# The down-projection of a two-mixer layer's MLP as seven half-sized products, accumulated and combined on VectorE

## The reference

```python
hn2 = rmsnorm(x, norm2_g[l])
up, ffn_new = causal_dwconv(hn2 @ w_up[l], st_ffn[l], ffn_conv_w[l])
a_f, b_f = jnp.split(up, [D_FF], axis=-1)
x = x + (jax.nn.silu(a_f) * b_f) @ w_down[l]
...
y = rmsnorm(x, norm_f_g)
```

## Time and profile before

| | before |
|---|---|
| median of 3 runs (lowest, highest) | 3739.96 us (3736.24, 3740.8) |
| profiled execution: time, span | 3742.75 us, 3741.0 us |
| mean granted TensorE clock | 0.979 of full speed |
| TensorE busy | 3574.4 us, 96% |
| VectorE busy | 2115.3 us, 57% |
| ScalarE busy | 710.3 us, 19% |
| GpSimd busy | 560.7 us, 15% |

### The profile page before, as it was taken

One profiled execution on the slowest core, in us unless ns is written; L12 is line 12 of the kernel. 1 busy time (PEld: TensorE's weight loads), 2 busy tenths in 40 slices (PEclk: granted clock), 3 DMA queues, 4 the chain that ended last, 5 costly groups with the idle time before them and its releaser, 6 DMA issues. The chain is left out here.

```text
span 3741.0 us, 49643 instructions
## 1 busy us (share of the span) xinstructions
PE 3574.4 (96%) x16817; PEld 2477.4 (66%) x16817; DVE 2115.3 (57%) x4957; ACT 710.3 (19%) x1564; POOL 560.7 (15%) x913
## 2 busy tenths in 40 slices
PE   7999999999999999999789999999989999999994
PEld 4666666666666666666567676767767777777772
DVE  2445555544455555445435656666666666666665
ACT  2222332222223322222111110101101111111112
POOL 1111100111110001111321111111132112112100
PEclk9999999999999999999779999999999999999997
DMA  5012221211122121111541111111131111111102
GB/s 194 23 46 67 67 67 56 67 47 47 52 67 67 58 65 60 45 40 60 159 149 34 50 34 47 37 45 39 34 126 52 34 40 39 39 34 45 39 22 101
DMA packets 202822, 224.04 MB, mean 60 GB/s; under 512 B 12764, under 2 KB 151556, under 8 KB 202771
## 3 DMA queue, kind: packets, MB, share of 16 engines
q1 hardware_dynamic: 202771, 223.37, 19.1%
HBM read 193.67 MB, written 29.67 MB: 60 GB/s over the span
## 5 line engine op out<-in xcount | busy, mean ns | idle before, releaser
L612 PE MATMUL mixer_bank<-arena,hnt 128*128 128x451 f32 x2176 | 923.7, 553 | 13.1 <-DVE yo L1227 9.5
L1846 PE MATMUL mlp_bank<-wd,act 128*128 128x512 f32 x1496 | 663.4, 596 | 21.2 <-DVE act L2086 21.2
L1787 PE MATMUL mlp_bank<-arena,ws 128*128 128x176 f32 (+1 forms) x3520 | 655.1, 339 | 0.2 <-ACT raw L1901 0.2
L1787 PEld LDWEIGHTS mlp_bank<-arena,ws 128*128 128x128 f32 x3520 | 587.9, 190 | 36.8 <-ACT raw L1901 0.5
L612 PEld LDWEIGHTS mixer_bank<-arena,hnt 128*128 128x128 f32 x2176 | 385.3, 191 | 302.8 <-issue 292.6
L1846 PEld LDWEIGHTS mlp_bank<-wd,act 128*128 128x128 f32 x1496 | 275.2, 186 | 354.2 <-issue 287.3
L549 POOL TENSOR_TENSOR ex<-dtt,level 128x512 f32<-128x512 f32 (+1 forms) x114 | 143.0, 1255 | 1150.6 <-DVE dtt L1432 740.2
L2072 DVE SCALAR_TENSOR_TENSOR mcv<-raw,cf,mcv 128x512 f32<-128x512 f32 (+2 forms) x440 | 289.6, 658 | 15.7
L2111 DVE TENSOR_TENSOR arena<-arena,mlp_bank 128x512 f32<-128x512 f32 (+1 forms) x396 | 263.9, 684 | 54.4 <-PE mlp_bank L1846 52.1
L628 PE MATMUL mixer_bank<-wo,th 128*128 128x512 f32 (+1 forms) x544 | 267.3, 615 | 6.4 <-DMA wo<-in_w_out_dram 6.4
L1787 PE MATMUL mlp_bank<-arena 128*128 128x176 f32 (+1 forms) x1320 | 253.4, 342 | 10.9 <-POOL ident_mlp L2008 10.1
(11 more groups left out here) (304 smaller groups left out, 3895.5 us busy)
## 6 DMA issues: line engine op xcount, KB each, us to landing
wo<-in_w_out_dram SPq DMA_DIRECT2D x272, 256.0 KB, 2.9
arena<-in_w_up_dram SPq DMA_DIRECT2D x44, 512.0 KB, 5.0
wu<-in_w_up_dram SPq DMA_DIRECT2D x44, 512.0 KB, 5.0
wd<-in_w_down_dram SPq DMA_DIRECT2D x44, 512.0 KB, 3.3
arena<-in_w_in_dram SPq DMA_DIRECT2D x8, 1804.0 KB, 17.3
xt<-in_x_prompt_dram SPq DMA_DIRECT2D x16, 512.0 KB, 3.3
xr<-in_x_prompt_dram SPq DMA_DIRECT2D x16, 512.0 KB, 3.4
resid<-yo SPq DMA_DIRECT2D x16, 512.0 KB, 3.5
```

The lines of the kernel that those rows point to most:

```text
L612: x = pe.matmul(bank[ring(g)][0:N, 0:GW], hnt[:, k, 0:N], w[:, k, g * GW:(g + 1) * GW], start=(k == 0), stop=(k == KT - 1))
L1787: x = pe.matmul(out[:, 0:N], left[:, k, :], xb[:, slot, k, g * N:(g + 1) * N], start=first and k == 0, stop=k == HK - 1, skip_group_check= ...
L1846: pe.matmul(bank[4 + (q + 2 * p * ps) % 4][0:N, :], act_[p][:, t * C:t * C + N], wd[p][:, e * 512:e * 512 + 512], start=True, stop=True).t ...
```

## The change

The down-projection is done for two steps at a time (a pair: steps 2i and 2i+1, 11 pairs in a pass). Over a pair the product is (1024 tokens x 256) by (256 x 1024); it is cut in halves in all three directions and done with seven products of half size each way instead of eight. So a pair has 28 products of the same shape as before instead of 32; the 32 sample tokens are left plain, two outputs of two accumulated products each. The 28 stand in pair i+1: 14 in its first step and 14 in its second.

The eight sums that this needs are on VectorE: `act_parts` (four, on 128 x 512 of the activations) and `weight_parts` (four, on 128 x 512 of the weights), put between the additions of `add` in the first step of a pair. The outputs accumulate over the pairs in seven sums, `acc`, which begin as three blocks of zeros and four of the residual, prepared by GpSimd (`start`). At the end of a pass they are combined (`combine`, seven additions): for half of the rows inside the last step, for the rest in `close`.

The last pair of a pass is plain: `close` does 16 (18) outputs of two products each, accumulated in PSUM, straight into the combined result. The final norm is now in both `close`s: ScalarE squares and scales tile by tile; the scaling on VectorE (`finish`) is in pass 1's `close` for its tiles, and for pass 0's in the first two steps of pass 1 (between the additions). The stores of pass 0 go out there as well. The transposes of the convolution tails (`turn_tails`) move into pass 1's `close`. `acc` takes the place of `y`; `act_` (four tiles now), `wd` and the sums are in the arena, and `wd` holds one pair.

```diff
+        PAIRS = FT // 2
+        OUTS = (28, 30)
+        CLOSING = (16, 18)
+        Q0 = (0, OUTS[0] * (PAIRS - 1) + CLOSING[0])
+        ORDER = (0, 1, 4, 5, 2, 6, 3, 7)
-        y_half = (sb("y", [C, TILES // 2, D]),
-                  arena[:, 0:(TILES // 2 + 1) * D].rearrange("p (t d) -> p t d", d=D))
+        acc = sb("acc", [C, 7, 4, 512])
+        y_sample = (sb("y_sample", [C, 512])[0:S, :], arena[0:S, 7808:8320])
+        act_ = [arena[:, i * PW:(i + 1) * PW] for i in range(4)]
+        act_sums = arena[:, 4224:5760].rearrange("p (i n) -> p i n", i=3)
+        wd_sums = arena[:, 5760:7808].rearrange("p (i n) -> p i n", i=4)
+        wd = [arena[:, 8320 + i * D:8320 + (i + 1) * D] for i in range(2)]
+        gf = act_sums[:, 0:2, :]
...
+            def down(ps, i):
+                if not (fixed(i, 1) and ps == 0):
+                    sp.wait_ge(s_down_done, first_out(ps, i))
+                for p in range(2):
+                    sp.dma_start(wd[p], w_down[bass.ds((2 * i + p) * C, C), :]).then_inc(s_wd_loaded, 16)
+
+            def start(ps):
+                if ps:
+                    sp.wait_ge(s_y_stored, 16 * 8)
+                for b in range(4):
+                    rows = slice(ps * T // 2 + b // 2 * 512, ps * T // 2 + b // 2 * 512 + 512)
+                    cols = slice(b % 2 * 512, b % 2 * 512 + 512)
+                    sp.dma_start(acc[:, 1 + b, :, :], resid[rows, cols].rearrange("(t p) d -> p t d", p=C))\
+                        .then_inc(s_acc_loaded, 16)
+                if ps:
+                    for e in range(2):
+                        sp.dma_start(y_sample[e], resid[T:T + S, e * 512:e * 512 + 512]).then_inc(s_acc_loaded, 16)
...
-                down(ps, FT - 1, 1)
+                up(ps, 3, 1)
+                with sp.Fori(2, PAIRS) as i:
+                    up(ps, sp.snap(2 * i), 0)
+                    up(ps, sp.snap(2 * i + 1), 1)
+                    down(ps, sp.snap(i - 1))
+                down(ps, PAIRS - 1)
+                sp.dma_start(gf, norm_f_g.partition_broadcast(C).rearrange("p (e d) -> p e d", e=2))\
+                    .then_inc(s_gf_loaded, 16)
+
+            def stores(ps):
+                for k, t in enumerate(ORDER):
+                    sp.wait_ge(s_f_out, 8 * ps + k + 1)
+                    r0 = ps * T // 2 + t * C
+                    sp.dma_start(y_p[r0:r0 + C, :].rearrange("p (e d) -> p e d", e=2), y_tile(t)).then_inc(s_y_stored, 16)
...
+            def down(ps, i, p, half, first, last):
+                a0, a1 = act_[2 * p], act_[2 * p + 1]
+                if first == 0 and half == 0:
+                    pe.wait_ge(s_act_made, group(ps, 2 * i + 1, PASSES[ps][1]))
+                    pe.wait_ge(s_wd_loaded, 32 * (PAIRS * ps + i + 1))
+                elif half == 0:
+                    pe.wait_ge(s_down_sums, 20 * ps + 2 * i + 2)
+                for o in range(14 * half + first, 14 * half + min(last, 14)):
+                    q, m = divmod(o, 7)
+                    lo, hi = slice(q * C, q * C + C), slice(512 + q * C, 512 + q * C + C)
+                    left, right = ((a0[:, lo], wd[0][:, 0:512]), (a1[:, lo], wd[1][:, 0:512]),
+                                   (act_sums[:, 2, lo], wd[1][:, 512:]), (a1[:, hi], wd_sums[:, 3, :]),
+                                   (act_sums[:, 0, lo], wd_sums[:, 0, :]), (act_sums[:, 1, lo], wd_sums[:, 1, :]),
+                                   (a0[:, hi], wd_sums[:, 2, :]))[m]
+                    bank_free(ps, i, o)
+                    pe.matmul(bank[4 + o % 4][:, :], left, right, start=True, stop=True).then_inc(s_down_done, 1)
+                if ps and half and last >= 14:
+                    for e in range(2):
+                        bank_free(ps, i, 28 + e)
+                        plain(bank[4 + e], 2 * p, 8, e, S)
+
+            def plain(out, a, t, e, N):
+                for j in range(2):
+                    x = pe.matmul(out[0:N, :], act_[a + j][:, t * C:t * C + N], wd[j][:, e * 512:e * 512 + 512],
+                                  start=(j == 0), stop=(j == 1))
+                x.then_inc(s_down_done, 1)
...
+            def close(ps):
+                i, o = PAIRS - 1, 0
+                pe.wait_ge(s_act_made, group(ps, FT - 1, 1))
+                pe.wait_ge(s_wd_loaded, 32 * PAIRS * (ps + 1))
+                for k, t in enumerate(ORDER + (8,) * ps):
+                    if k == 2:
+                        pe.wait_ge(s_act_made, group(ps, FT - 1, PASSES[ps][1]))
+                    for e in range(2):
+                        bank_free(ps, i, o)
+                        plain(bank[4 + o % 4], 2 * (i % 2), t, e, S if t == 8 else C)
+                        o += 1
+                    if ps and k in (1, 3, 5):
+                        turn_tails(k // 2)
+
+            def pair(ps, i, p):
+                up(ps, 2 * i if isinstance(i, int) else pe.snap(2 * i), 0, lambda: down(ps, i - 1, 1 - p, 0, 0, 2))
+                down(ps, i - 1, 1 - p, 0, 2, 14)
+                up(ps, 2 * i + 1 if isinstance(i, int) else pe.snap(2 * i + 1), 1,
+                   lambda: down(ps, i - 1, 1 - p, 1, 0, 2))
+                down(ps, i - 1, 1 - p, 1, 2, 14)
...
+            def start(ps):
+                if ps:
+                    gp.wait_ge(s_combined, 21 * ps)
+                for m in (1, 6, 7):
+                    x = gp.memset(acc[:, m - 1, :, :], 0.0)
+                x.then_inc(s_acc_step, 1)
+                gp.wait_ge(s_acc_loaded, 64 + 96 * ps)
+                gp.wait_ge(s_acc_step, ps + 1)
+                gp.tensor_tensor(acc[:, 2, :, :], acc[:, 2, :, :], acc[:, 4, :, :], ALU.subtract).then_inc(s_acc_ready, 1)
...
+            def act_parts(ps, i, p):
+                lo, hi = slice(0, 512), slice(512, 1024)
+                step = 5 * (10 * ps + i)
+                a0, a1 = act_[2 * p], act_[2 * p + 1]
+                dve.wait_ge(s_act_made, group(ps, 2 * i + 1, PASSES[ps][1]))
+                dve.tensor_tensor(act_sums[:, 0, :], a0[:, hi], a1[:, hi], ALU.add).then_inc(s_sums_step, 1)
+                dve.wait_ge(s_sums_step, step + 1)
+                dve.tensor_tensor(a0[:, hi], a0[:, lo], a0[:, hi], ALU.subtract).then_inc(s_sums_step, 1)
+                dve.tensor_tensor(act_sums[:, 1, :], act_sums[:, 0, :], a0[:, lo], ALU.subtract).then_inc(s_sums_step, 1)
+                dve.wait_ge(s_sums_step, step + 3)
+                dve.tensor_tensor(act_sums[:, 2, :], a1[:, lo], act_sums[:, 1, :], ALU.subtract).then_inc(s_down_sums, 1)
+
+            def weight_parts(ps, i):
+                lo, hi = slice(0, 512), slice(512, 1024)
+                step = 5 * (10 * ps + i) + 3
+
+                def first():
+                    dve.wait_ge(s_wd_loaded, 32 * (PAIRS * ps + i + 1))
+                    dve.tensor_tensor(wd_sums[:, 0, :], wd[0][:, hi], wd[0][:, lo], ALU.subtract).then_inc(s_sums_step, 1)
+                    dve.tensor_tensor(wd_sums[:, 2, :], wd[1][:, hi], wd[0][:, hi], ALU.subtract)
+
+                def second():
+                    dve.wait_ge(s_sums_step, step + 1)
+                    dve.tensor_tensor(wd_sums[:, 1, :], wd[1][:, hi], wd_sums[:, 0, :], ALU.subtract)\
+                        .then_inc(s_sums_step, 1)
+                    dve.wait_ge(s_sums_step, step + 2)
+                    dve.tensor_tensor(wd_sums[:, 3, :], wd[1][:, lo], wd_sums[:, 1, :], ALU.subtract)\
+                        .then_inc(s_down_sums, 1)
+                return (first,), (second,)
+
...
+            def combine(ps, n, q0, q1, steps):
+                v = [None] + [acc[:, m, q0:q1, :] for m in range(7)]
+                n += 21 * ps
+                for k in steps:
+                    to, by, done = ((6, 1, 0), (2, 1, 0), (7, 6, 1), (6, 5, 3), (3, 6, 4), (4, 7, 3), (5, 7, 4))[k]
+                    if k == 0:
+                        dve.wait_ge(s_y_added, first_out(ps, PAIRS - 2) + 14 * (q0 // 2 + 1))
+                    if done:
+                        dve.wait_ge(s_combined, n + done)
+                    dve.tensor_tensor(v[to], v[to], v[by], ALU.add).then_inc(s_combined, 1)
+
...
+            def close(ps):
+                n, o = first_out(ps, PAIRS - 1), 0
+                order = ORDER + (8,) * ps
+                for k, t in enumerate(order):
+                    N = S if t == 8 else C
+                    if k in (0, 4, 6):
+                        dve.wait_ge(s_combined, 21 * ps + (7, None, None, None, 14, None, 21)[k])
+                    for e in range(2):
+                        dve.wait_ge(s_down_done, n + o + 1)
+                        if o == 0:
                             dve.wait_ge(s_y_added, n)
-                        v = y_half[ps][0:N, t, e * 512:e * 512 + 512]
-                        dve.tensor_tensor(v, v, bank[4 + (q + 2 * p * ps) % 4][0:N, :], ALU.add)\
-                            .then_inc(s_y_added, 1)
+                        v = half_acc(t, e, N)
```

(19 more changed lines are left out.)

282 lines of the change are left out of this document (148 added, 134 removed).

## The result

| | before | after |
|---|---|---|
| median (lowest, highest) | 3740.38 us (3736.24, 3741.06), 4 runs | 3650.07 us (3649.07, 3652.91), 4 runs |
| ratio, 95% interval | | 0.9762, 0.9745 to 0.9779 |
| profiled execution: time, span | 3742.75, 3741.0 us | 3652.91, 3651.2 us |

The forecast was 3641 us with a range of 3619 to 3668, so the time lies in the range and 9 us above the forecast. The direction and most of the size are right. The question is where the 9 us are, and whether the terms were right or errors cancelled.

The account below looks back on a forecast made before the run. TensorE was taken to bound the loops, with standing at the passes' ends. Terms -68.9 + 1.4 - 0.9 + 7 - 37.9 = -99.3 us from 3742.75 give 3643.5, median 2.8 us lower: 3641 us, range 3619 to 3668.

Parts of the forecast that it names:

- Parts 1 and 2: Loops: four products fewer a pair save 68.9 us; VectorE's added sums cost 1.4 us of waiting in pass 1's second group.
- Part 3: VectorE operations with two SBUF inputs and GpSimd's SBUF reads exclude each other for a whole instruction; a sum takes 2.06 us.
- Part 4: End of pass 0: weights wait 4.9, slow clock 2.4, combinings 9, ScalarE 1, less 18.2 us; together -0.9 us.
- I take 9 us: Pass 0's `close`: cost of VectorE's 14 combining additions at 2.06 us beside GpSimd's sums, ends 0 and 14.
- The 1 us for ScalarE: Between the passes: ScalarE squares pass 0's last tile before it copies pass 1's first product, 1 us.
- the prediction's own sign: Wrong if TensorE waits over 1 us a pair in loops, or pass 0's `close` ends off VectorE's count.
- Part 5: Beginning of each pass, +7 us: pass 1's collisions with GpSimd 5, scalings of pass 0's tiles 1, pass 0's start 1.
- Part 6: End of the kernel: 56.5 us becomes 18.6, -37.9 us (ends -42 and -31), with 7.5 to the last scaling, 3.8 for the store.
- No collision at the ends: Rival, 15%: at the passes' ends VectorE's combining finds GpSimd idle and the clock stays up; 3622 us.
- VectorE paces pass 1: Rival, 17%: the second group's 0.1 us margin fails and the wait passes through convolution and gate; 3664 us.
- The products save nothing: Rival, 3%: in the loops TensorE waits for free banks instead, so only the end is won; about 3709 us.
- the likeliest case: The forecast itself for the whole kernel, 3641 us, given 63%; its own range 3626 to 3656 us.

## Why the prediction was right, and where its terms were off

**Parts 1 and 2, products and VectorE in the loops.** Right in mechanism and size: 68.7 against 68.9 us, pairs of 72.38 and 77.90 against 72.4 and 78.2. The 1.4 us of waiting in pass 1's second group (for nine pairs; there are ten) did not come; there is 0.33 us of room where the prediction had 0.1, and the run with two sums more shows that this place, not the load of 72%, would have decided.

**Part 3, GpSimd against VectorE.** Confirmed by the runs: 1.89 us for three combinings without the input sums, 5.14 with them. The Trainium skill, "SBUF — State Buffer", section "Who interferes with whom", has a VectorE instruction with two SBUF inputs and a GpSimd instruction that reads SBUF exclude each other for a whole instruction; the 4.49 us for 32 columns beside a subtraction of 4.83 us agree.

**Part 4, the end of pass 0.** The wait for the weights was 5.15 us (4.9 forecast) and the slow clock behind it 3.3 us (2.4): 48 halves in 23.86 us, at 0.4293 us each 20.6. The step "I take 9 us" for the combinings was too high: they took 1.52 us each (21.27 us for fourteen) where the prediction took 2.06 for all. The first of each group took 0.68 to 0.98 us, and only the eight behind it 1.64 to 2.16; TensorE waited 2.55 us, lost 1.9 to the clock behind it (8.79 us for 16 halves, 6.87 at 0.4293 us each), 4.5 in all, and leaving the sums out gave 4.6. The 1 us for ScalarE does not show at pass 1's first product. The rest was -5.3 instead of -0.9. By the prediction's own sign (`close` ends earlier than VectorE's count says) this part was wrong in size: VectorE's count was 39 us, and 21.3 + 10 = 31 came.

**Part 5, the beginnings of the passes, is the term that failed.** "5 us, ends 0 and 12" for pass 1 and "1 us" for pass 0. Measured, with part 2, 21.6 us instead of 8.4. The step was "in 53 to 55, GpSimd's subtraction to 60": it timed the start of the sums by the residual's landing. In the trace GpSimd's queue sets it: `keep` of the second step waits for VectorE's last addition (row at 2803.75, 15.21 us idle), and then zeroings and subtraction follow without a gap, 5.46 + 4.83 us; the residual, issued at 2792.88, was there in time. The zeroings had no price in the prediction, and the convolution of the second step, which TensorE's third step wants, falls right beside them and the subtraction; the prediction had put `act_parts` there and the convolution beside the weight sums, and it came the other way round. In pass 0 the same happens, though its residual is there early: that reason for "1 us" was beside the point. Taking the work off GpSimd gave back about 5 us in pass 0 and 6 in pass 1. Beside the 6.58 us pass 1 has costs of its own: 1.52 us at its second product, which comes from the close (0.42 us without the input sums), 1.12 us at 2790.32 behind a scaling of 2.04 us (1.28 in pass 1's close), 4.4 us at the turns of VectorE's loop, which the prediction didn't have, 2.1 us for the two waits behind the 6.58, and 1.35 of slow clock. That makes 17.1 us; less the 3 us that the ten pairs gave beyond their products, 14 of the 15.7 are found.

**Part 6, the end.** -34.3 instead of -37.9. VectorE was quicker than the 7.5 us taken (4.4), but "3.8 us for the store" was 9.1: the order of SyncE's queue was not read, though it stands in the code. With the stores first it is 4.0 us. The three transposes of the tails, now between products in `close`, had no term: TensorE's next product starts 0.65 us after the start of each, 2 us in all.

**The rivals.** No collision at the ends: wrong, the collisions are there. VectorE paces pass 1: not by this change, but 1 us more would have done it. The products save nothing: a pair is shorter by all of its four products. So the likeliest case was right. That the total was nearer than its terms is in part luck: pass 0's close and the unchanged first part were 7.5 us better than forecast while the passes' beginnings and the end were 16.8 us worse. Measured again, the kernel was 14 us above the forecast, still in its range.

## What to carry to other kernels

When set-up work is put on an idle engine, time it by that engine's queue, with what stands before and behind it, and not by its input; splitting its instructions frees the neighbour but not the queue. A transfer moved to just before a place where the bound engine waits is worth its full time only until the next wait, so look up what that is first. Price an end by the last engine's queue of stores, in its order. A loop that goes over twice as many steps may pay at each turn: compare the packets of the instruction queues before and after.

## What was not expected of the hardware

- VectorE's TENSOR_SCALAR on float32 in SBUF was held by GpSimd's MEMSET (2.89 us, 0.39 usual; 4.55 us beside twelve short ones), though a MEMSET reads nothing; two SCALAR_TENSOR_TENSOR of 128 x 512 at 1979.63 us, with two SBUF inputs, ran in their usual 1.54 us beside one that began at 1979.70. Beside the subtraction, which reads SBUF, the same operation was held (4.49 us for 32 columns).
- VectorE's turn of a loop of four steps costs it 2.4 to 2.7 us (three times in each pass; TensorE feels it only in pass 1), which the loop of two steps before did not show; written out, it is gone.
- TensorE's clock fell behind short waits too: to 0.79 in the window 1995 to 2003, behind 3.45 us, and behind 2.55 us at 2739.38 (16 halves in 8.79 us, 7.03 usual). The length of the wait alone doesn't decide it: with the stores first a wait of 2.54 us at the same place was followed by 8 halves in 3.70 us, the usual rate.
- SyncE needed 1.3 us to issue each 512 KB store of an output tile (10.42 us for eight; 0.87 each for the two at 3638.01 in the kernel with the stores first), so eight stores in a row are a stretch of work of their own.
